# 128 extra matmuls with differing moving-operand layouts, put ahead of the first query unit

## The reference

```python
z = rmsnorm(x, g_attn) @ w_in            # split into q_a, k_a, v_a, q_m, x_b, g_b
o_a = chunk_band_attention(q_a, k_a, v_a)        # 8 heads x 128
o_m = softmax_attend(q_m, mem_k, mem_v)          # 4 heads x 128 over 256 memory rows
o_b = rg_lru(causal_dwconv(x_b)) * gelu(g_b)     # width 512
x = x + concat(o_a, o_m, o_b) @ w_out
up = causal_dwconv3(rmsnorm(x, g_ffn) @ w_up)    # 2 x 6144
x = x + (gelu(gate) * val) @ w_down
```

## Time and profile before

| what | value |
|---|---|
| median of the two runs | 2312.99 us |
| the two runs | 2312.77 and 2313.22 us |
| span of the profiled execution, first to last instruction | 2310.7 us |
| PE busy | 2303.2 us, 18000 instructions |
| DVE busy | 1780.9 us |
| ACT busy | 1156.9 us |
| POOL busy | 307.2 us |
| HBM traffic over the span | 134 GB/s |

### The profile page before, as it was taken

One profiled execution on the slowest core, in us unless ns is written; L12 is line 12 of the kernel. 1 busy time (PEld: TensorE's weight loads), 2 busy tenths in 40 slices (PEclk: granted clock), 3 DMA queues, 4 the chain that ended last, 5 costly groups with the idle time before them and its releaser, 6 DMA issues.

```text
span 2310.7 us, 44975 instructions
## 1 busy us (share of the span) xinstructions
PE 2303.2 (100%) x18000; PEld 2284.7 (99%) x18000; DVE 1780.9 (77%) x2410; ACT 1156.9 (50%) x1885; POOL 307.2 (13%) x258
## 2 busy tenths in 40 slices
PE   9999999999999999999999999999999999999999
PEld 8999999999999999999999999999999999999999
DVE  6788667665424888888888888888888988786876
ACT  4566454454322555555555455545555555454543
POOL 5100000000112111111121121111211110000000
PEclk9999999999999999999999999999999999999999
DMA  9522333332533434434343344343434678687864
GB/s 295 150 83 78 110 90 89 106 89 83 176 102 115 113 111 133 120 116 137 112 141 117 118 126 127 111 140 111 139 116 146 174 198 208 157 206 161 214 146 102
DMA packets 479142, 309.87 MB, mean 134 GB/s; under 512 B 10841, under 2 KB 457177, under 8 KB 478953
## 3 DMA queue, kind: packets, MB, share of 16 engines
q1 hardware_dynamic: 470520, 289.97, 42.6%
q0 software_dynamic: 8432, 17.27, 4.6%
HBM read 255.79 MB, written 53.51 MB: 134 GB/s over the span
## 4 chain that ended last, share of the span: by engine, by line
PE 63%; DVE 3%; issue 1%; ACT 0%; DMA 0%; DVEq 0%; ACTq 0%
PE out L2688 21%; PE out L2690 21%; PE out L2689 21%; DVE ring_l L1995 1%; DVE fl L2229 0%; DVE t L1988 0%; ACT ring_h L1403 0%; DVE pair L2022 0%; DVE s_buf L2005 0%; DVE out L2093 0%; DVE pair L2029 0%; DMA out_yT<-rows 0%; ACT t L1382 0%; DVE rows L2159 0%; DVE rows L2176 0%
## 5 line engine op out<-in xcount | busy, mean ns | idle before, releaser
L1995 DVE TENSOR_TENSOR ring_l<-pair,ring_h 128x1024 fp32r<-128x1024 f32 (+1 forms) x384 | 455.7, 1187 | 178.2 <-ACT ring_h L1403 178.1
L1403 ACT CAST ring_h<-pair 128x1024 fp32r<-128x1024 f32 (+1 forms) x384 | 383.0, 998 | 321.9 <-DVE pair L2022 228.0
L2688 PE MATMUL out<-t,ring_h 128*128 128x272 f32 x1536 | 443.8, 289 | 1.1 <-DVE ring_l L1995 0.6
L2690 PE MATMUL out<-t,ring_l 128*128 128x272 f32 x1536 | 444.1, 289 | 0.0
L2321 PE MATMUL out<-xh,wh 128*128 128x272 f32 x1600 | 442.7, 294 | 0.0
L2689 PE MATMUL out<-t,ring_h 128*128 128x272 f32 x1536 | 441.9, 288 | 0.0
L2322 PE MATMUL out<-xl,wh 128*128 128x272 f32 x1600 | 431.5, 288 | 0.0
L2688 PE MATMUL out<-fh,ring_h 128*128 128x272 f32 x1344 | 387.6, 288 | 2.3 <-DVE ring_l L1995 1.6
L2690 PE MATMUL out<-fh,ring_l 128*128 128x272 f32 x1344 | 387.5, 288 | 0.0
L2689 PE MATMUL out<-fl,ring_h 128*128 128x272 f32 x1344 | 386.3, 287 | 0.0
L2324 PE MATMUL out<-xh,wl 128*128 128x272 f32 x1600 | 331.8, 289 | 0.0
(11 more groups left out here) (287 smaller groups left out, 3960.2 us busy)
## 6 DMA issues: line engine op xcount, KB each, us to landing
pair<-in_w_up SPq DMA_DIRECT2D x192, 512.0 KB, 3.9
raw<-in_w_in SPq DMA_DIRECT2D x36, 1024.0 KB, 5.5
pair<-in_w_down SPq DMA_DIRECT2D x64, 384.0 KB, 4.5
pair_d<-in_w_down SPq DMA_DIRECT2D x64, 384.0 KB, 4.5
h_forms<-fb SPq DMA_DIRECT2D x24, 816.0 KB, 6.0
fr<-h_forms SPq DMA_DIRECT2D x24, 816.0 KB, 6.7
out_yT<-stage POOLq DMA_DIRECT2D x31, 544.0 KB, 7.8
raw<-in_w_out SPq DMA_DIRECT2D x16, 1024.0 KB, 5.9
```

The lines of the kernel that those rows point to most:

```text
L1403: nc.scalar.copy(ring_h[:, n % 3, 0:width(i)], weight_of(p, i)).then_inc(op_hi, 1)
L1995: v.tensor_tensor(ring_l[:, n % 3, 0:w], weight_of(p, i), ring_h[:, n % 3, 0:w].bitcast(F32), ALU.subtract).then_inc(op_lo, 1)
L2688: mm(out, w_high, high[:, k, :], start=opens and k == 0, stop=False, skip_group_check=True)
L2690: ins = mm(out, w_low, high[:, k, :], start=False, stop=k == tiles - 1, skip_group_check=True)
```

## The change

A function `layouts` is added to TensorE's block and called once, behind the last memory unit and ahead of unit `U_QX`. It issues 22 groups of matmuls, 20 of six and two of four. All are F32R, all write `means[:, 0, 0:n]` with `start=True, stop=True`, and all read `xl[:, 7, 0:128]` as weights (one group reads `xl[:, 7, 8:136]`). Fourteen groups have 272 columns, six have 256, two have 512. The moving operand is read from `xh` and differs in its first element, its step (0, -1, 2), and its blocks (16 or 4 elements, next to each other, spaced, or alternating between two places 2176, 2180 or 2192 elements apart). Two waits stand ahead: `xlo` at `K8` = 8, and `roots_ready` at `N_XROWS` = 5. Nothing is removed or moved.

```diff
             for u in range(3, U_QX):
                 mem_unit(u, mem_between(u))
 
+            def layouts():
+                w = xl[:, 7, 0:P]
+                w_off = xl[:, 7, 8:P + 8]
+                row = KT * ROWS
+
+                def high(first, *pattern):
+                    return bass.AP(xh, first, [[row, P], *pattern])
+
+                def plain(first, n):
+                    return xh[:].rearrange("p k n -> p (k n)")[:, first:first + n]
+
+                def apart_lines(distance, block):
+                    return high(0, [block, N_MEM // 2 // block], [distance, 2], [1, block])
+
+                half = HALF
+                operands = [
+                    [(plain(0, half), w)] * 6,
+                    [(plain(4, half), w)] * 6,
+                    [(plain(8, half), w)] * 6,
+                    [(plain(12, half), w)] * 6,
+                    [(plain(32, half), w)] * 6,
+                    [(plain(48, half), w)] * 6,
+                    [(high(0, [0, half]), w)] * 6,
+                    [(high(half - 1, [-1, half]), w)] * 6,
+                    [(high(0, [2, half]), w)] * 6,
+                    [(high(0, [16, half // 16], [1, 16]), w)] * 6,
+                    [(high(0, [32, half // 16], [1, 16]), w)] * 6,
+                    [(plain(0, half), w_off)] * 6,
+                    [(plain(0, half), w), (plain(8, half), w)] * 3,
+                    [(plain(0, half), w), (plain(half, half), w)] * 3,
+                    [(plain(0, N_MEM), w)] * 6,
+                    [(apart_lines(8 * HALF, 16), w)] * 6,
+                    [(apart_lines(8 * HALF, 4), w)] * 6,
+                    [(apart_lines(8 * HALF + 16, 16), w)] * 6,
+                    [(apart_lines(8 * HALF + 4, 4), w)] * 6,
+                    [(plain(8, N_MEM), w)] * 6,
+                    [(plain(0, 512), w)] * 4,
+                    [(plain(8, 512), w)] * 4,
+                ]
+                for group in operands:
+                    for moving, weights in group:
+                        n = 1
+                        for _, count in moving.ap[1:]:
+                            n *= count
+                        mm(means[:, 0, 0:n], weights, moving, start=True, stop=True)
+
+            pe.wait_ge(xlo, K8)
+            pe.wait_ge(roots_ready, N_XROWS)
+            layouts()
+
             for m in range(HM):
                 u = U_QX + 2 * m
```

## The result

The changed kernel takes 2329.91 us (two runs, 2329.55 and 2330.26) against 2312.99: ratio 1.0074, interval 1.0045 to 1.0103. 2329.7 was forecast.

What follows compares the result with a forecast made beforehand. TensorE was taken to bound the kernel; 10.54, 1.87 and 4.32 us of inserted matmuls made 16.7, so 2310.7 + 16.7 + 2.3 between span and median gave 2329.7 us. Own range 2328.5 to 2331.5, wider 2327.5 to 2335.

Steps and rivals of the forecast that it cites:

- The bound: Whole kernel: TensorE bounds it, busy 2303.2 of 2310.7 us, with no idle time where the matmuls are inserted.
- the two waits: Ahead of the inserted groups: `xlo` and `roots_ready` are met 5.7 us or more earlier, so both cost nothing.
- the part behind: After the insertion: no engine takes the time back; later work moves along by the same 16.7 us.
- The sum: Inserted matmuls before the first query unit: 84 x 125.5, 36 x 120 and 8 x 233.3 ns, 16.7 us together.
- The likeliest case: Whole kernel: the insertion adds 16.7 us, most groups costing what contiguous rows cost; 2329.7 us.
- Rival 1: Inserted groups: hopping reads are slow, limited by 16-byte pieces, so step 2 needs twice the pieces; 18.5 to 30 us, chance 0.2.
- Its bundle of four groups: In rival 1: step 2, step -1 and two groups with alternating blocks of 4 double; 2.9 us more, 2332.6.
- Rival 2: Inserted matmuls: self-contained F32R on one bank can't be pipelined; 37.7 us, chance 0.02; slower by over 2%, chance 0.01.
- Rival 3: Inserted matmuls: they don't run, dropped as dead work by the build; 2313.0 us, chance 0.02.
- Rival 4: Inserted groups: all layouts at the clock's rate, or idle given back downstream; 2327.3 to 2328.3 us, chance 0.12.
- The clue: F32R streams in the kernel before: 8% behind the clock, which looks like a limit in reading the moving operand.

Runs made afterwards that it cites:

- experiment 8: Changed kernel's inserted groups replaced by groups of F32R, bf16 at several steps, both formats in turn, and float32 with F32R; 2364.78 us in one run.
- experiment 9: Kernel before, without the insertion; second and third product of every split product read constant bf16 operands and weights; 2290.70 us, ratio 0.9904.

## Why the prediction was right

**The bound, the two waits and the part behind.** Right, and shown: the waits alone cost 0.15 us within an interval of 2 us either way, the unit started at 82.56 us, inside the 81 to 84 that were named, and the time grew by 16.97 and 32.32 us when TensorE's stretch grew by 16.87 and 32.27.

**The sum.** The mechanism and nearly all of the size are right: the terms of 272 columns (125.5 taken, 124 to 127 contiguous), of 256 (120 taken, 119 to 120) and of 512 (233.3 taken, 232 to 234) stood. The likeliest case lacked one term. In the trace the stretch was 17.57 us instead of 16.7, and of the 0.87 us the step-2 group is 0.7 (242 ns instead of 125.5, six times), the format step that changed place 0.1, and the two groups of alternating blocks of 4 about 0.1. That the measured time still met 2329.7 within 0.2 us is partly luck: two runs of each kernel and a place of insertion that moves by some tenths of a us between executions can't tell 0.7 us. The forecast range of 15.7 to 18.5 us holds either value.

**Rival 1** was true in its first half. Step 2 doubles; step -1 (125 to 127 ns) doesn't, nor do the alternating blocks of 4, which cost 6 to 8% more. The reason it gave, that twice the 16-byte pieces are read, fits step 2 and every other pattern with up to 136 lines; for F32R steps from 3 up, four times the pieces cost no more than twice. Its bundle of four groups held one that doubles, and its 18.5 to 30 us began above the 17.57 that came.

**Rival 2** is refuted: self-contained F32R matmuls on one bank follow each other at 125 to 127 ns. **Rival 3** is refuted by the 128 instructions in the trace. **Rival 4**: only step 0 came near the clock's rate, and its reason (changing weights) fell with the contiguous groups, which kept 125 to 127 ns with one and the same weight tile.

**The clue** was right for the greater part, and that part is now shown. A contiguous F32R stream needs a 16-byte line every four columns, 4 x 0.417 = 1.67 ns, and from 272 to 512 columns a line takes 1.77: (232 - 125.5) / 60 lines. That it is the line's time is shown by step 0 (no new lines, 0.417 ns a column), by bf16 (half the lines, 116 ns), by the bf16 steps, where 68 to 272 lines take 1.75 to 1.78 ns each, and by the clock level that doesn't matter to them. Lines don't explain all of it: with the same 68 lines bf16 takes 120 ns and F32R 125.5, and with step 0 F32R takes 119 where bf16 at step 1 takes 116. So 3 to 6 ns of a matmul's 9.7 above 115.8 go with the format, and why stays open.

The Trainium skill, TensorE: Matmul & The Clock Gate, Back-to-back issue gap, gives N/2.4 + 2.5 ns, 115.8 and 215.8 ns for 272 and 512 columns at the full clock, and calls it the gap of an isolated matmul. For 512 columns in a stream with weight loads it gives about 131 ns. The prediction took the formula for that of a stream. The streams here agree with the formula for contiguous bf16 (116, and 216 in experiment 8) and differ from it for contiguous F32R (125.5, 232); no stream of 512 columns came near 131.

The Trainium skill, SBUF — State Buffer, in the remark on cachelines, names 16-byte lines and says two hits a line are enough for the full rate. The runs bear out the lines and not the two hits: F32R step 2 (two hits) and bf16 step 4 (two hits) run at half rate, bf16 step 2 (four hits) at 120 ns.

## What to carry to other kernels

Price an insertion into a queue that never idles by the distance between starts of its nearest kin, and expect the whole time to grow by that sum. Divide a group by its count only where the next group has the same format; otherwise look at its last start. Count the 16-byte lines of a moving operand: contiguous F32R is just bound by them (8% over the clock, most of it lines), anything that touches two lines for four F32R columns runs at half rate, while offsets, reversal and gaps between whole lines are nearly free. Half-width operands buy the 8% back only in long runs of one format, and only if the engines that make them have slack where TensorE would wait.

## What the runs showed of the hardware

- A bf16 or float32 moving operand costs 1.75 to 1.78 ns for each new 16-byte line, or the clock's rate of 0.417 ns a column at 2.4 GHz (float32 twice that), whichever is longer: 116, 120, 181, 242, 299, 358 and 480 ns for bf16 steps 1, 2, 3, 4, 5, 6 and 8. At bf16 step 8 it was 480 ns at both clock levels. Float32 step 8, also 272 lines, stands a little above, at 490 ns.
- F32R has an exception that stays open: from step 3 up it costs 231 to 258 ns for 272 columns (step 15 was the dearest) and not the 480 ns of 272 lines that float32 and bf16 pay.
- A turn from bf16 to F32R costs 15 to 18 ns, which ate four fifths of the gain of experiment 9. The F32R matmul is seen to start 30 to 50 ns behind the start of the bf16 one before it.
- The granted clock fell to 0.50 while TensorE was issuing without pause, but at 480 ns for 272 columns. Before that it had stood at full through a group of 242 ns; a later float32 group of 479 ns an instruction kept the full clock. In experiment 8 it stood at 0.50 behind six bf16 matmuls of 480 ns.
